# Single k-tiles of the first two projection groups between the pieces of the modulation product

## What is computed

```python
shift, scale, gate = jnp.split((jax.nn.silu(c) @ w_mod + b_mod)[:, None, :], 3, axis=-1)
shift_c, scale_c, gate_c = jnp.split(jax.nn.silu(c_ctx) @ w_mod + b_mod, 3, axis=-1)
h = modulate(x, norm_w, shift, scale)            # rms_norm(x) * norm_w * (1 + scale) + shift
hc = modulate(ctx, norm_w, shift_c, scale_c)
aq, ak, av, az, ab, aa, bq, bk, bv, bz, br = split_in(h @ w_in)
```

## Time and profile before

| | us |
|---|---|
| median of three executions | 2053.45 |
| lowest and highest | 2053.30 and 2053.74 |
| the profiled execution: span from the first to the last instruction | 2050.0 |
| the profiled execution's own time beyond its span | not shown by the page |

### The profile page before, as it was taken

How to read it: one execution, slowest core, us unless ns; L and a number is a source line. 1 busy time by engine, 2 the same in 40 slices (tenths; PEclk the granted TensorE clock), 3 DMA queues, 4 the chain that set the end, 5 groups by cost and what they waited for, 6 DMA issues and landing times.

```text
span 2050.0 us, 39188 instructions
## 1 busy us (share of the span) xinstructions
PE 1942.2 (95%) x17278; PEld 1521.1 (74%) x17278; DVE 939.4 (46%) x1823; ACT 620.4 (30%) x1057; POOL 231.1 (11%) x385
## 2 busy tenths in 40 slices
PE   5679999999999999999999999899999889999999
PEld 2138888888777777777887877778887566678887
DVE  1323343565334555445445445575435644354333
ACT  4313222223143333222332322442235333322121
POOL 0000000000022222211112211311100101110000
PEclk9999999999999999999999999999999999999999
DMA  8872121223232222222221222667633222464333
GB/s 310 297 236 62 52 62 54 60 82 87 62 93 59 60 73 67 60 64 64 73 64 53 64 64 74 201 217 228 204 113 114 82 87 85 161 213 133 118 118 103
DMA packets 159474, 229.28 MB, mean 112 GB/s; under 512 B 10352, under 2 KB 108905, under 8 KB 157897
## 3 DMA queue, kind: packets, MB, share of 16 engines
q1 hardware_dynamic: 136841, 157.14, 25.9%
q0 software_dynamic: 14688, 55.48, 8.1%
q10 hardware_dynamic: 7776, 14.16, 1.9%
HBM read 203.15 MB, written 23.59 MB: 111 GB/s over the span
## 4 chain that ended last, share of the span: by engine, by line
PE 83%; DMA 6%; ACT 5%; DVE 4%; issue 2%; POOL 1%; SPq 0%; ACTq 0%; DVEq 0%; POOLq 0%
PE psum L1390 22%; PE psum L1392 20%; PE psum L1391 20%; DMA w_raw_mod<-w_mod_dram 3%; PE psum L1668 2%; PE psum L1457 2%; PE psum L1453 2%; PE psum L1514 1%; ACT inv L671 1%; PE psum L1465 1%; DVE w_lo L898 1%; PE psum L1420 1%; PE psum L1688 1%; PE psum L1655 1%; ACT w_hi L605 1%
## 5 line engine op out<-in xcount | busy, mean ns | idle before, releaser
L898 DVE TENSOR_TENSOR w_lo<-w_raw,w_hi 128x1024 fp32r<-128x1024 f32 x232 | 290.6, 1253 | 579.5 <-ACT w_hi L605 579.1
L605 ACT ACTIVATE w_hi<-w_raw 128x1024 fp32r<-128x1024 f32 x232 | 245.4, 1058 | 991.4 <-PE psum L1392 949.6
L1390 PE MATMUL psum<-h_hi,w_hi 128*128 128x512 f32 x1152 | 482.1, 419 | 13.8 <-DVE w_lo L898 11.6
L1392 PE MATMUL psum<-h_hi,w_lo 128*128 128x512 f32 x1152 | 454.1, 394 | 0.0
L1391 PE MATMUL psum<-h_lo,w_hi 128*128 128x512 f32 x1152 | 453.1, 393 | 0.0
L1390 PEld LDWEIGHTS psum<-h_hi,w_hi 128*128 128x128 f32 x1152 | 217.7, 189 | 56.2 <-DVE w_lo L898 8.3
L1392 PEld LDWEIGHTS psum<-h_hi,w_lo 128*128 128x128 f32 x1152 | 217.2, 189 | 50.5
L1391 PEld LDWEIGHTS psum<-h_lo,w_hi 128*128 128x128 f32 x1152 | 218.5, 190 | 33.0
L968 DVE SCALAR_TENSOR_TENSOR conv_acc<-conv_in,convw,conv_acc 128x772 f32<-128x772 f32 x96 | 98.2, 1023 | 3.4
L1390 PE MATMUL psum<-w_hi,m_hi 128*128 128x512 f32 x256 | 99.6, 389 | 0.0
L1391 PE MATMUL psum<-w_lo,m_hi 128*128 128x512 f32 x256 | 99.6, 389 | 0.0
(11 more groups left out here) (307 smaller groups left out, 2907.5 us busy)
## 6 DMA issues: line engine op xcount, KB each, us to landing
w_raw<-w_in_dram SPq DMA_DIRECT2D x168, 512.0 KB, 3.8
w_raw_mod<-w_mod_dram SPq DMA_DIRECT2D x64, 512.0 KB, 5.6
w_raw_modg<-w_mod_dram POOLq DMA_DIRECT2D x32, 512.0 KB, 4.4
w_raw<-w_out_dram SPq DMA_DIRECT2D x32, 512.0 KB, 3.7
gate_scratch<-gate_stage ACTq DMA_DIRECT2D x48, 256.0 KB, 3.9
w_raw<-w_proj_a_dram SPq DMA_DIRECT2D x16, 512.0 KB, 3.9
w_raw<-w_proj_b_dram SPq DMA_DIRECT2D x16, 512.0 KB, 3.7
gates<-gate_scratch POOLq DMA_DIRECT2D x32, 256.0 KB, 4.0
```

What stands on the lines that cost most here:

```text
L605: act.activation(part(whi[i % 2], p), part(place, p), ACT.Copy).then_inc(S("w_hi"), 1)
L898: dve.tensor_tensor(part(wlo[i % 2], p), part(raw_of(n)[0], p), part(whi[i % 2], p).bitcast(f32), ALU.subtract).then_inc(S("w_lo"), 1)
L1390: pe.matmul(out_ap, lh, rh, start=first, stop=False, skip_group_check=shared)
L1392: return pe.matmul(out_ap, ll, rh, start=False, stop=last, skip_group_check=shared)
```

## The change

The list of pieces is no longer group by group at its start. Five pieces of the first two `conv` groups (groups 8 and 9 of the whole list) are set in behind modulation pieces m = 31, 39, 47, 55 and 63, and the two groups' last three pieces follow. New numbers: m = 31 is n = 31 and the early piece n = 32; m = 63 is n = 67 and its early piece n = 68; then 69 (third piece of group 9), 70 and 71 (last pieces of 8 and 9). Group 10 begins at n = 72.

On TensorE an early piece is done in four single k-tiles: the first three behind m - 6, m - 4 and m - 2 (m the modulation piece ahead of it), the fourth at the piece's own n. So from m = 25 on every second modulation piece is followed by a k-tile. Its load is issued behind that of m - 8, its split is done at the iteration of m - 10. Piece 69 is split at the iteration of m = 59 and loaded behind m = 61.

Moved with it: the x tiles now come every third n (X_AT = 1, 4, 7, 10, 13, 16), `H_AT` becomes 21, 33, 51 and 68, the last block's high and low parts are done in the same iteration as its columns, as is `mod_columns` of the last group; the modulation accumulates in banks 6 and 7 (with its columns in the same bank, once it has been copied), so that banks 0 to 5 serve the two `conv` groups; the work behind groups 9 and 10 comes two and one n later (`late`).

```diff
+EARLY = {31: (0, 0), 39: (1, 0), 47: (0, 1), 55: (1, 1), 63: (0, 2)}
...
+    pieces = []
+    for i, p in enumerate(p for g in own[:8] for p in g):
+        pieces.append(p)
+        if i in EARLY:
+            group_of, quarter = EARLY[i]
+            pieces.append(own[8 + group_of][quarter])
+    pieces += [own[9][2], own[8][3], own[9][3]]
+    pieces += [p for g in own[10:] for p in g]
+    for gi, g in enumerate(groups):
+        at = [n for n, p in enumerate(pieces) if p["g"] == gi]
+        g["first"], g["last"] = at[0], at[-1]
+        g["late"] = {9: 2, 10: 1}.get(gi, 0)
...
+    mods_made = np.cumsum([p["kind"] == "mod" for p in PIECES]).tolist()
+    MOD_AT = [n for n in range(NP) if PIECES[n]["kind"] == "mod"]
+
+    EARLY_AT = [MOD_AT[m] + 1 for m in EARLY]
+    BEFORE_LAST = {MOD_AT[m - 6 + 2 * kk]: (MOD_AT[m] + 1, kk) for m in EARLY for kk in range(3)}
+    SPLIT_AT = [n - 1 for n in range(NP)]
+    for m in EARLY:
+        SPLIT_AT[MOD_AT[m] + 1] = MOD_AT[m - 10]
+    SPLIT_AT[MOD_AT[63] + 2] = MOD_AT[59]
+    LOADS = []
+    for n in range(NP):
+        if n not in EARLY_AT and n != MOD_AT[63] + 2:
+            LOADS.append(n)
+        LOADS += [MOD_AT[m] + 1 for m in EARLY if n == MOD_AT[m - 8]]
+        LOADS += [MOD_AT[63] + 2] * (n == MOD_AT[61])
...
-    X_AT = [1 + 4 * t for t in range(NT)]
+    X_AT = [1 + 3 * t for t in range(NT)]
     H_AT = [max(g["last"] + 2, X_AT[-1] + 5) for g in MODS if g["scale"]]
+    H_AT[-1] -= 1
+    H_PARTS_AT = [a + 1 for a in H_AT[:-1]] + [H_AT[-1]]
+    MODV_AT = [g["last"] + 2 for g in MODS[:-1]] + [MODS[-1]["last"] + 1]
...
             g = GROUPS[gi]
             if g["kind"] == "mod" and gi >= 2:
-                eng.wait_ge(S("mod_rows"), gi - 1)
+                eng.wait_ge(S("mod_evac"), gi - 1)
...
-            for n, p in enumerate(PIECES):
-
-                before = n - 4 if n < NM else n - 2
-                if before >= (0 if n < NM else NM):
+            for n in LOADS:
+                p = PIECES[n]
+                if p["kind"] == "mod":
+                    m = mods_made[n] - 1
+                    before = MOD_AT[m - 4] if m >= 4 else None
+                else:
+                    r = n - mods_made[n]
+                    before = RING_AT[r - 2] if r >= 2 else None
+                if before is not None:
...
             for n in range(N_PA0):
-                hi_part(n + 1)
+                for m in range(NP):
+                    if SPLIT_AT[m] == n:
+                        hi_part(m)
...
-                    if n == H_AT[j] + 1:
+                    if n == H_PARTS_AT[j]:
                         h_hi_parts(j)
...
-                    e = n - g["last"]
+                    e = n - g["last"] - g["late"]
...
-                for kk in range(p["nk"]):
+                for kk in ks or range(p["nk"]):
                     k = p["k0"] + kk
                     st, sp_ = first and kk == 0, last and kk == p["nk"] - 1
-                    if gi == G_CONV0:
+                    if gi in (G_CONV0, G_CONV0 + 1):
                         pe.wait_ge(S("h_lo"), 2 * (k + 1))
...
             for n in range(N_PA0):
-                piece(n)
+                piece(n, ks=(3,) if n in EARLY_AT else None)
+                if n in BEFORE_LAST:
+                    early, kk = BEFORE_LAST[n]
+                    piece(early, ks=(kk,))
...
                     if n == g["last"] + 1:
-                        if gi >= 2:
-                            pe.wait_ge(S("mod_evac"), gi - 1)
                         mod_cols(mrow, 6 + gi % 2, "mod", gi + 1)
```

More of the change, by code:

```diff
@@ L60, in shape_constants @@
     return consts, rope
+EARLY = {31: (0, 0), 39: (1, 0), 47: (0, 1), 55: (1, 1), 63: (0, 2)}
 def projection_plan():
-    groups, pieces = [], []
+    groups, own = [], []
     def group(kind, col, width, per_piece, **more):
[L69 to L73, removed]
+        own.append([dict(g=len(groups), kind=kind, k0=k0, nk=per_piece, col=col, width=width)
+                    for k0 in range(0, more.get("kt", KT), per_piece)])
+        groups.append(dict(kind=kind, col=col, width=width, **more))
     for j in range(4):
@@ L93, in projection_plan @@
         group("out", 512 * j, 512, 2, j=j)
+    pieces = []
[10 more added lines that the diff above has]
+        g["late"] = {9: 2, 10: 1}.get(gi, 0)
+    assert len(pieces) == sum(len(g) for g in own)
     return groups, pieces
@@ L155, in build @@
     SPLIT = [n for n in range(NP) if not whole[n]]
+    mods_made = np.cumsum([p["kind"] == "mod" for p in PIECES]).tolist()
[12 more added lines that the diff above has]
+        LOADS += [MOD_AT[63] + 2] * (n == MOD_AT[61])
+    assert sorted(LOADS) == list(range(NP))
+    RING_AT = [n for n in range(NP) if PIECES[n]["kind"] != "mod"]
     MODG = [dict(k0=2 * (q // 4), nk=2, col=2 * DM + 512 * (q % 4), width=512, kind="mod") for q in range(32)]
@@ L358, in raw_of @@
         def raw_of(n):
-            if n < NM:
-                return raw_mod[n % 4], S(f"w_in_mod{n % 4}"), 16 * (n // 4 + 1)
-            return raw[n % 2], S(f"w_in{n % 2}"), 16 * ((n - NM) // 2 + 1)
+            if PIECES[n]["kind"] == "mod":
+                m = mods_made[n] - 1
+                return raw_mod[m % 4], S(f"w_in_mod{m % 4}"), 16 * (m // 4 + 1)
+            r = n - mods_made[n]
+            return raw[r % 2], S(f"w_in{r % 2}"), 16 * (r // 2 + 1)
         def accs_free_needed(eng, gi):
@@ L899, in lo_part @@
                                   ALU.subtract).then_inc(S("w_lo"), 1)
-            for b in (4, 5):
+            for b in (6, 7):
                 dve.memset(bank(b), 0.0).then_inc(S("rows_zero"), 1)
@@ L1167, in _ @@
             for n in range(N_PA0):
-                lo_part(n + 1)
+                for m in range(NP):
+                    if SPLIT_AT[m] == n:
+                        lo_part(m)
                 for t in range(NT):
@@ L1173, in _ @@
                         x_norm(t)
-                for gi, g in enumerate(MODS):
-                    if n == g["last"] + 2:
+                for gi in range(len(MODS)):
+                    if n == MODV_AT[gi]:
                         mod_columns(gi)
@@ L1344, in _ @@
             pe.wait_ge(S("rows_in"), 96)
-            pe.transpose(bank(7, 97), rows[:], ident[0:97, 0:97]).then_inc(S("rowsT"), 1)
-            pe.transpose(bank(6, 120), crows[:], ident[0:120, 0:120]).then_inc(S("rowsT"), 1)
+            pe.transpose(bank(0, 97), rows[:], ident[0:97, 0:97]).then_inc(S("rowsT"), 1)
+            pe.transpose(bank(1, 120), crows[:], ident[0:120, 0:120]).then_inc(S("rowsT"), 1)
             def x_transposes(t):
@@ L1472, in gdn, with piece @@
                     ins.then_inc(S(f"gp{d}"), 1)
-            def piece(n, halves=(0, 1)):
+            def piece(n, halves=(0, 1), ks=None):
                 p = PIECES[n]
@@ L1491, in piece @@
                     return
-                if first:
+                if first and (not ks or ks[0] == 0):
                     accs_free_needed(pe, gi)
@@ L1507, in piece @@
                         return
-                    b0 = 4 + gi % 2
+                    b0 = 6 + gi % 2
                     if first and gi < 2:
@@ L1578, in piece @@
                             ins = three(bank(b0 + t), l, (wh[:, kk, :], wl[:, kk, :]), st, sp_)
-                if kind != "gate":
+                if kind != "gate" and kk == p["nk"] - 1:
                     ins.then_inc(S("w_used"), 1)
```

11 lines of the change are left out of this document (6 added, 5 removed).

## The result

| | before | after |
|---|---|---|
| median of four executions | 2053.59 | 2026.93 |
| lowest to highest | 2053.30 to 2057.13 | 2023.38 to 2028.35 |
| span of the profiled execution | 2050.0 | 2026.5 |

The ratio is 0.9865 with a 95% interval of 0.9845 to 0.9885: 26.7 us less, against 24.9 forecast (2028.5, range 2018 to 2039). On another occasion the changed kernel took 2024.77 (ratio 0.9857, 0.9844 to 0.9871).

What follows compares the result with a forecast made beforehand. Modulation is bound by weight transfers, what follows by TensorE. Piece 25 at 76.2 plus 78.9 gives 155.1 against 180.7, 25.6 less; a 0.7 stall leaves 24.9 net: median 2028.5, range 2018 to 2039.

Steps and rivals of the forecast that it cites:

- What bounds what: Modulation stage bound by weight transfers, what follows by TensorE; matmuls moved into the first are worth their time there.
- The 180.7: End of the five pieces before the change, from the stretch 138.25 to 180.66; taken as up to 0.8 too late.
- The start of piece 25: ScalarE's queue of squares, split and h block delays modulation rows; piece 25 at 76.2 instead of 72.67.
- From piece 25 on: TensorE's k-tiles, modulation pieces and column steps, 73.9 us, with changeovers and late transfers: 78.9 us from piece 25's start.
- The 0.96: On TensorE, 0.96 us for a modulation piece before a k-tile, against 0.43 before another modulation piece.
- The 3 us for late transfers: In the modulation stage, buffers freed late and queueing behind additional loads: 3 us, between 0 and 13.
- Hidden on average, by 7.5 us: From piece 25 on, 40 transfers at 1.66, 66.4 us, lie beside TensorE's 73.9 us.
- Behind the stage: After the last early k-tile, a stall of 0.7 us before piece 70, between 0 and 3; nothing at piece 72.
- A: Start of piece 25: no one holds TensorE, piece 25 near 69.8 and singles don't queue; 2019, chance 0.15.
- B: Modulation stage: the ring is held, pairs take 4.2 instead of 3.51, 13 us in place of 3; 2038.5, chance 0.20.
- C: Modulation stage: the transfer stream stands still during each k-tile; 24 us slower, 2077, chance 0.02.
- D: All 20 early k-tiles run at half clock, costing 42.4 us more; time near 2071, chance 0.02.

Runs made afterwards that it cites:

- The two experiments on ScalarE's order: Changed kernel with the first h block ahead of the first early split: 2019.77; or only its high and low parts behind the third modulation rows: 2020.06.
- one product: Changed kernel with only high by high made in the 20 early k-tiles, 4 matmuls instead of 12: 2017.16 in one execution.

## Why the prediction was right

By its own steps, in their order.

**What bounds what.** Right. The gain is the five pieces' 42.4 us less what the modulation stage grew by. The 180.7 was read wrongly: it is 138.25 and 42.4, without the columns step that lies inside. The seventh split of weights, which waits for the fifth piece, is at 181.8, so 180.7 is 1.1 too early, and not up to 0.8 too late; in the changed kernel the step follows the five pieces and takes 0.8 of that back. Counting the splits of the weights from the first, the eighth is 25.7 us earlier than before (190.3 to 164.6) and the 25th 26.7 (345.0 to 318.3). The 1 us between them is not the columns step that the prediction spoke of: that step lies ahead of the eighth split in both kernels (146.9 and 155.0). Projection pieces with no other work between them follow each other by 8.40 us in the traces of the changed kernel and by 8.48 in the other, which over 17 pieces makes up that 1 us; why is open. At the end it is 23.5 by the profiled executions; 2.3 are lost between 1765 and 1789 us of the changed kernel, which had a granted clock of 0.87 from 1775 to 1785 where the other had 1.00. I take that for most of the cause and did not test it.

**The start of piece 25: right in kind, 4.7 us too early (76.2 against 80.9).** The timeline of ScalarE has the order that the prediction put down:

```profile
53.70 2.06 ACT L662 ACTIVATE xnT<-psum 128x512 f32<-128x512 f32 x4 [2.27 <-PE psum L1401]
56.40 1.91 ACT L652 ACTIVATE junk<-x_rows 128x2048 f32<-128x2048 f32 x1 [0.64 <-DMA x_rows<-ctx_dram]
...
58.31 0.58 ACT L775 ACTIVATE mod_rows<-psum 128x512 f32<-128x512 f32 x1
...
72.05 1.06 ACT L646 ACTIVATE w_hi<-w_raw 128x1024 fp32r<-128x1024 f32 x1 [4.55 <-DMA w_raw<-w_in_dram]
75.18 0.63 ACT L668 ACTIVATE h_hi<-xnT 128x512 fp32r<-128x512 f32 x1 [2.07 <-DVE xnT L987]
...
78.50 0.57 ACT L775 ACTIVATE mod_rows<-psum 128x512 f32<-128x512 f32 x1
```

The square of tile 5 (56.40) stands ahead of the second modulation rows (58.31), and the first early split (72.05) and four pairs of high parts ahead of the third (78.50, against 70.94 in the earlier trace rows; 74.6 forecast). TensorE waited for both:

```profile
58.94 1.87 PE L1408 MATMUL psum<-consts,mod_rows 128*128 128x2 f32 x8 [3.96 <-ACT mod_rows L775]
...
64.25 2.51 PE L1401 MATMUL psum<-consts,x_rows 128*128 128x128 f32 x16
...
79.13 1.86 PE L1408 MATMUL psum<-consts,mod_rows 128*128 128x2 f32 x8 [3.74 <-ACT mod_rows L775]
80.92 1.87 PE L1559 MATMUL psum<-w_raw_mod,silu_c 128*2 128x512 f32 x4
82.72 0.80 PE L1435 MATMUL psum<-h_hi,w_hi 128*128 128x512 f32 x1
...
86.46 1.04 PE L1559 MATMUL psum<-w_raw_mod,silu_c 128*2 128x512 f32 x8
```

The second modulation rows at 58.31 (57.7 forecast), the third columns step at 79.13 (75.2), tile 5 at 64.25 (60.5). The step that was mis-sized is the landing of the first early load, at 72.05 instead of 68. SP issued it at 64.77, when piece 19 had been used; piece 19 started at 62.40, just ahead of tile 5's transposes, and the pieces 17 to 19 stood 0.8 to 0.9 us apart instead of 0.43, at the lower clock, behind the wait at 58.94. The half-clock stretch behind piece 24 adds the rest: a columns step takes 1.8 instead of 1.0, and the first k-tile 3.74 (82.72 to 86.46) instead of 2.31. The two experiments on ScalarE's order show that this queue is the cause: by the traces each had the eighth split of weights 5 us earlier (164.6 to 159.6 and 159.9), and the medians fell by 7, 2026.93 to 2019.77 and to 2020.06, across two series.

**From piece 25 on: 74.1 us against 78.9.** Twenty k-tiles and 39 modulation pieces were counted rightly. A pair with its k-tile took 3.28, where the terms (0.43, 0.96, 2.12 and 0.1) made 3.61. The 0.96 from a single piece to a full-width operation was read rightly, but it counts from the first of two pieces; this is 0.43 too much, 19 times, and was partly made up by 0.09 too little for each k-tile (2.31 to the next pair, against 2.12 and 0.1) and by the lower clock at the start of the stage, which no term held: 1.8 us from piece 25 to the first k-tile instead of 0.96, and 3.74 for that k-tile. The 3 us for late transfers were also about right: TensorE's waits for modulation weights in front of matmuls from 80 to 152 us sum to 3.4. This error and that of piece 25 cancel: 155.0 against a forecast 155.1 for the end of the last k-tile. The total is that near by luck of two signs, not by two exact terms.

**"Hidden on average, by 7.5 us."** This step failed, without harm. With one product the stage takes 72.0 us, so the slack was at most 2, not 7.5, and from piece 26 to piece 63 there was none (66.9 us against 65.4). The price of a transfer was not the fault: nine of them take 14.4 to 14.8 us in that kernel, 1.60 to 1.64 each, where 1.66 was put down. The 7.5 compared whole stages, and most of it is the four pieces that are in the ring when the stage starts: 4 x 1.66 = 6.6 us. For a group of eight the prediction's own terms give TensorE 4 x 3.51 + 1.0 = 15.1 us and nine transfers 14.9. Nor was that head start to be had: with the ring full and TensorE held, the DMA engines stood still from 79 to 82 us, a share of 0.00 in both traces, and the next weights were a landing away.

**Behind the stage.** Piece 70 started 0.2 us late (164.58, against the last matmul of piece 69 at 164.27 and its 0.12); 0.7 forecast. TensorE had no wait at piece 72.

**The rivals.** A needed piece 25 at 69.8; what it would give was then built, by moving work on ScalarE and VectorE: piece 25 at 68.4 and 2016.73, where A had 2019. Its other half, that singles don't queue, was not seen. B's mechanism is real and its price lies in the length of the block: with single k-tiles it cost no more than the 3 us put down, in twos 6.7 us on top, in fours all 26. C did not come, but the whole pieces are close to it: there the change is worth nothing, at 4.95 us for two pieces and a k-tile (19.8 / 4), and the prediction had put the point at 5.1. D: the clock. The granted clock was 0.51 from 72 to 84 us, where TensorE waited, and 1.00 once k-tiles stood between the pieces; only the first k-tile ran at the lower level. The rule that I had quoted from the Trainium skill, page TensorE: Matmul & The Clock Gate, section "HAM oscillation — how this bites in real kernels", is about short bursts with DMA waits between them. The trace has 1.00 over 62 us, where those waits are nearly gone (3.4 us in all), so it does not test the rule; with whole pieces, where they came back (3.39 us and others), the granted clock was 0.90 over the same 62 us, lower but far from half.

## What to carry to other kernels

Where one stretch waits for transfers and the next for matmuls, work can be moved across, but it must be cut fine: what the transfers lose grows with how long the engine that frees their buffers is away, and here the same work won 30.4 us with one k-tile at a time, 23.7 with two (same series) and 0.2 with four. Before forecasting such a move, follow the queues of the engines that prepare the first moved piece: the squares, the split and the h block that stood ahead of a short step which TensorE waited for cost 8 us of the 38 that were to be had. And compare two limits over one period of the steady stage, not over the stage with its ends: over the whole they seemed 7.5 us apart, over a group of eight 0.1.

## What the runs showed of the hardware

A full-width matmul behind two two-column pieces started 0.97 us after the first of them and 0.54 after the second (97.08 and 97.51 to 98.05); behind a single one it was 0.96 (151.87 to 152.83). So the 0.96 is no fixed price for every piece ahead. A ring of four transfers of 512 KB moved 315 GB/s with every buffer used at once (84 to 134 us before the change), and 331 GB/s with six transfers of a second ring among 33 of the first (88 to 150 us after it). After a block in which the ring had run dry, the next piece's weights came 5.3 us behind the first use that freed their buffer (98.49 to 103.78), where a landing takes 5.1 in the full stretch: a dry ring costs a whole landing again. And the same kernel, with nothing changed, took from 2046 to 2062 us in 19 executions, more than the whole 8 us that the order on ScalarE was worth.
